# Who issues the 32 copies that double the keys: GpSimd, or ScalarE behind its weight conversions

## The reference

```python
q, kc, vc, ks, vs, kw, vw, gl = jnp.split(h @ w_in, splits, axis=-1)
kc, ks, kw = [partial_rope(to_heads(t, G), cos, sin) for t in (kc, ks, kw)]
# compressed branch: blocks of 32 tokens through a small MLP
return jax.nn.gelu(blk @ w1) @ w2            # once for kc, once for vc
# selected branch: softmax(q . ks) @ vs; window branch: softmax(q . kw) @ vw
o = gb[:, 0] * o_c + gb[:, 1] * o_s + gb[:, 2] * o_w
```

## Time and profile before

| | |
|---|---|
| median of 3 runs | 2381.58 us (2381.36 to 2381.64) |
| the profiled execution | 2382.09 us, of which its span is 2380.3 us |
| PE busy | 2370.0 us |
| PEld busy | 2002.1 us |
| DVE busy | 1332.7 us |
| ACT busy | 899.4 us |
| POOL busy | 310.5 us |
| mean granted TensorE clock | 0.999 |
| attention prologues (ACT's first copy of a high key half to the transposes on PE) | 53.5 to 113.5 us in layer 0, 1706.1 to 1772.3 us in layer 3 |

### The profile page before, as it was taken

The page is one execution under the profiler, slowest core; times in us unless marked ns, Lnnn a source line. Parts: engine busy times, 40 slices in busy tenths (PEclk is TensorE's granted clock), DMA queues, the critical chain, the costliest instruction groups (busy, mean ns, idle before and its releaser), DMA issues.

```text
span 2380.3 us, 33586 instructions
## 1 busy us (share of the span) xinstructions
PE 2370.0 (100%) x11768; PEld 2002.1 (84%) x11768; DVE 1332.7 (56%) x2199; ACT 899.4 (38%) x1376; POOL 310.5 (13%) x305
## 2 busy tenths in 40 slices
PE   9999999999999999999999999999999999999998
PEld 7899988888888888888888888888889998888887
DVE  8667765344465764443586644446756676534444
ACT  6267833222233432222233322223426773322223
POOL 2211140000040120000033000003420114000003
PEclk9999999999999999999999999999999999999999
DMA  4710023232233232322233223233370002223232
GB/s 165 224 46 2 2 69 108 88 101 93 99 105 106 89 106 91 103 97 97 97 99 106 97 91 104 89 106 105 121 208 27 2 2 89 97 89 106 89 105 89
DMA packets 64616, 220.58 MB, mean 93 GB/s; under 512 B 7680, under 2 KB 7808, under 8 KB 64512
## 3 DMA queue, kind: packets, MB, share of 16 engines
q1 hardware_dynamic: 58320, 208.59, 26.3%
q0 software_dynamic: 5184, 8.40, 1.6%
q10 hardware_dynamic: 1008, 2.21, 0.3%
HBM read 208.68 MB, written 2.10 MB: 89 GB/s over the span
## 4 chain that ended last, share of the span: by engine, by line
PE 99%; DVE 0%; DMA 0%; ACT 0%; SPq 0%; issue 0%; DVEq 0%
PE bank L1516 95%; PE bank L1796 3%; DMA x<-x_in 0%; PE bank L1826 0%; DVE branch L1281 0%; DVE big L1509 0%; SPq L434 0%; DVE rden L1276 0%; ACT L588 0%; DVE w_lo L939 0%; DVE rden L1278 0%; ACT w_hi L572 0%; PE bank L1700 0%; ACT xs_hi L581 0%; ACT xg L907 0%
## 5 line engine op out<-in xcount | busy, mean ns | idle before, releaser
L1516 PE MATMUL bank<-xs_hi,w_hi 128*128 128x512 f32 (+1 forms) x1808 | 708.9, 392 | 1.1 <-DVE xs_lo L947 0.5
L1516 PE MATMUL bank<-xs_lo,w_hi 128*128 128x512 f32 (+1 forms) x1808 | 703.3, 389 | 0.0
L1516 PE MATMUL bank<-xs_hi,w_lo 128*128 128x512 f32 x1792 | 697.3, 389 | 0.0
L939 DVE TENSOR_TENSOR w_lo<-raw,w_hi 128x1024 fp32r<-128x1024 f32 x369 | 469.7, 1276 | 230.7 <-ACT w_hi L572 226.3
L572 ACT ACTIVATE w_hi<-raw 128x1024 fp32r<-128x1024 f32 x372 | 390.8, 1051 | 432.6 <-PE bank L1516 231.7
L1516 PEld LDWEIGHTS bank<-xs_hi,w_hi 128*128 128x128 f32 (+1 forms) x1808 | 339.0, 188 | 74.4 <-DVE xs_lo L947 1.5
L1516 PEld LDWEIGHTS bank<-xs_lo,w_hi 128*128 128x128 f32 (+1 forms) x1808 | 338.4, 187 | 71.0 <-issue 1.0
L1516 PEld LDWEIGHTS bank<-xs_hi,w_lo 128*128 128x128 f32 x1792 | 336.4, 188 | 70.0
L1516 PE MATMUL bank<-hid_hi,w_hi 128*128 128x512 f32 x720 | 280.5, 390 | 0.0
L1516 PE MATMUL bank<-hid_lo,w_hi 128*128 128x512 f32 x720 | 280.1, 389 | 0.0
L1516 PE MATMUL bank<-hid_hi,w_lo 128*128 128x512 f32 x720 | 280.1, 389 | 0.0
(11 more groups left out here) (212 smaller groups left out, 2719.8 us busy)
## 6 DMA issues: line engine op xcount, KB each, us to landing
raw<-stream SPq DMA_DIRECT2D x371, 512.0 KB, 3.2
w_f<-stream SPq DMA_DIRECT2D x18, 512.0 KB, 3.5
hid_hi<-mix_hi POOLq DMA_DIRECT2D x32, 128.0 KB, 3.7
hid_lo<-mix_hi POOLq DMA_DIRECT2D x32, 128.0 KB, 3.1
out<-big SPq DMA_DIRECT2D x8, 256.0 KB, 2.9
x<-x_in ACTq DMA_DIRECT2D x4, 256.0 KB, 6.8
x<-x_in SPq DMA_DIRECT2D x4, 256.0 KB, 7.5
big<-consts SPq DMA_DIRECT2D x1, 664.0 KB, 11.0
```

The source lines that it names most:

```text
L939: nc.vector.tensor_tensor(w_lo[:, slot, :], raw[:, k, :], f32(w_hi[:, slot, :]), ALU.subtract).then_inc(w_lo_ready, counted(b))
L1516: return nc.tensor.matmul(out_, w, v, start=start, stop=stop)
```

## The change

The 32 copies of a layer leave POOL's list and go to ACT's. ACT issues them in its loop over blocks 8 to 23, four at a time, behind the conversion of that turn: for key tile i (0 to 3) the high half in turn j = 10 + 4i, the low half in j = 11 + 4i. The wait for the stage is kept; POOL's waits on `block_done`, which spaced its groups, have no successor. Source, destination (as float32 on both sides) and count of the copies are the same.

```diff
-                for j in range(KS, MIXED):
-                    for stage, key, ready in ((stage_hi, key_hi, stage_hi_ready), (stage_lo, key_lo, stage_lo_ready)):
-                        gp.wait_ge(ready, 4 * a + j - KS + 1)
-                        gp.wait_ge(block_done, plan.mix[l] + MIXED + 2 * (2 * (j - KS) + (stage is stage_lo)) - 2)
-                        for half in range(2):
-                            for h in range(2):
-                                gp.dma_start(key[64 * h:64 * h + 64, (j - KS) // 2, 2 * (j % 2) + half, :],
-                                             stage[64 * half:64 * half + 64, j - KS, :]).then_inc(key_full, 16)
...
+                def copies(j, stage, key, ready):
+
+                    act.wait_ge(ready, 4 * a + j - KS + 1)
+                    for half in range(2):
+                        for h in range(2):
+                            act.dma_start(f32(key[64 * h:64 * h + 64, (j - KS) // 2, 2 * (j % 2) + half, :]),
+                                          f32(stage[64 * half:64 * half + 64, j - KS, :])).then_inc(key_full, 16)
+
                 for j in range(MIXED, GATE):
                     split_after(B + j, (B + j) % RING)
                     if j < MIXED + 2:
                         post(j - 2)
+                    if (j - MIXED) % 4 == 2:
+                        copies(KS + (j - MIXED) // 4, stage_hi, key_hi, stage_hi_ready)
+                    if (j - MIXED) % 4 == 3:
+                        copies(KS + (j - MIXED) // 4, stage_lo, key_lo, stage_lo_ready)
                     if j == W1_AT[3] + 1:
                         hidden(0)
                     if j == W1_AT[3] + 4:
```

## The result

| | before | after |
|---|---|---|
| median | 2381.64 us (2381.26 to 2382.77, 20 runs) | 2385.47 us (2383.34 to 2390.97, 20 runs) |
| profiled execution | 2382.09 us | 2385.04 us |

The ratio is 1.0017, 95% interval 1.0011 to 1.0023. The kernel became slower by 3.8 us. That is inside 0.2%, but four times the loss of 0.9 us that was forecast (2382.5 us), and 0.3 us above the upper end of the range. Its runs also scatter more, 7.6 us against 1.5 us.

The account below looks back on a forecast made before the run. PE, busy 2370.0 of 2380.3 us, was taken as the bound. Waits of 0.77 us (layer 0) and 0.16 (layer 3), all else 0, gave 2382.09 + 0.93 = 2383.0 for the profiled execution, median 2382.5; range 2381.1 to 2385.2 us.

Parts of the forecast that it names:

- the place: Low half of key tile 3, between block 26's conversion and `hidden(1)`: PE waits 0.77 us in layer 0, 0.16 in layer 3.
- the three cases of the start: Group behind an ACTIVATE: issues start with it (taken), when it has ended (1.06 us later), or without waiting for its load.
- the rival of no stall: Deciding group issued while block 26's conversion still waits for its load; `hidden(1)` starts at 112.70 as before; 2381.6 us, chance 0.20.
- that of the late start: Deciding group waits for the ACTIVATE's end; PE loses 1.83 and 1.22 us, sum 3.05; 2384.6 us, chance 0.26.
- The other groups: Groups elsewhere in ACT's prologue list fall into its idle time, even eight issues behind block 21's conversion; cost 0.
- the last copies: Issued by about 113.6, landing at 117.1 to 121.0 against ACT's wait ahead of 120.47; worst case 0.5 us, not needed soon.
- The slower rival: Deciding group starts late and each issue costs ACT 0.70 us; 5.0 us lost, 2386.6 us, chance 0.07.
- the text's own signs of being wrong: PE waiting for `w_lo` or a score, layer 3's wait as long as layer 0's, or issues ahead of the conversion.
- The issue's price: Four copies on ACT: 0.34 us for the first, 0.50 for each other, 1.84 a group; ends 1.3 and 2.8.
- The copies' bytes: High half of tile 3, ahead of block 26's load: 0.5 MB need 1.4 us in a 2 us hole; cost 0.
- The range's upper end: 2385.2 us: the late start plus 0.6 us for a load that lands later.
- a loss of clock: TensorE's clock falling behind PE's stall would add time, but a stall of 2 us doesn't seem enough; no size given.

Follow-up runs that it names:

- high_behind: Changed kernel with the high half of key tile 3 issued behind `hidden(1)` instead of ahead of block 26's load; 2383.27 us, ratio 1.0006.
- eight: Changed kernel with the high half of key tile 3 moved to turn 23, so eight issues instead of four precede `hidden(1)`; 2389.94 us, ratio 1.0036.
- twelve: Changed kernel with twelve issues ahead of `hidden(1)` in turn 23: low half of tile 2, both halves of tile 3; 2398.06 us, ratio 1.0068.
- pool_late: Kernel before, copies on GpSimd, only the high half of key tile 3 issued later, behind the low half; 2381.85 us, ratio 1.0000.
- low_ahead: Changed kernel with the low half of key tile 3 ahead of block 26's conversion, right behind the high half; 2384.39 us, ratio 1.0012.
- pool_late_two: Kernel before, copies on GpSimd, both halves of key tile 3 issued late, when VectorE is done with block 24; 2384.21 us, ratio 1.0011.
- gelu_first: Changed kernel with `hidden(1)` ahead of turn 23's four copies, still behind block 26's conversion; 2382.24 us, ratio 0.9999.

## Why the prediction was right and wrong

Right were the place and one mechanism: the group between block 26's conversion and `hidden(1)`, with PE waiting for `tmp` twice and nowhere else in the two prologues. So was the choice among the three cases of the start: the issues begin with the ACTIVATE (111.99 and 111.98), not at its end and not while it waits for its load. With that the rival of no stall and that of the late start fell; the rule on the wait queue that stood behind the first, in the Trainium skill's page "Perfetto Trace Analysis", section "DVE / Act Engine Instruction (TENSOR_ADD, Activation, etc)", didn't hold for DMA issues behind a waiting ACTIVATE: the data of the copies had long been there, and the first issue still came only at the end of ACT's idle 7.72 us. The other groups cost nothing, as said; `hidden_turned(0)` and block 25 made nobody wait, and no wait is for the last copies. The slower rival's price of 0.70 an issue didn't hold either (0.62).

One of the text's own signs of being wrong nearly came: a wait in layer 3 as long as in layer 0. It had 0.16 against 0.77 us; measured were 1.48 and 1.64. The issues are the same in both layers, so what made the two alike is m, that is the load.

Three steps were off.

**The issue's price, a term mis-sized.** "I take 0.34 for the first of a group and 0.50 for each of three more, 1.84 us a group." The group in question took 2.42 and 2.41 us, 0.47 for its shortest issue and 0.62 for the median one. The nearest rows, loads from HBM on the same queue, were lower than the copies' price on ACT. POOL's for the very copies (0.52) were nearer, and even they too low. With the margins of before, 1.76 and 2.37, the need of 2.96 would make PE stand 1.20 and 0.59 us, 1.8 in all, where the text had 0.93. high_behind, with the same need and m of 2.25 and 2.46, measured 1.5 us above before. A smaller error hid part of this one, by luck: the text took the start of PE's weight load, 113.26, for the moment at which PE wants `hidden(1)`. The stalls fit the transposes' start, 113.49, less 0.05. By that the text's own 1.84 us a group would have given 0.59 us in layer 0 and nothing in layer 3.

**The copies' bytes, taken as 0.** This is the larger miss, and the step that failed: "there is a hole of 2 us for these 0.5 MB, and at the 381 GB/s of the full window they need 1.4. I take 0." 381 GB/s was the rate of the weights' loads. Where copies fill the DMA engines the traces show 194 GB/s at a share of 0.81 (before) and 213 at 0.94 (after), which makes 2.5 us of these 0.5 MB. And they are later than in that reckoning: the issues take 3.01 us, from 103.20 to 106.21. So they overlap SP's loads from 106.3 on. What that does to m, in the ten layers of the five profiled kernels with the high half there and in the ten of five without it (before, eight, high_behind, twelve and the kernel before with the GELU ahead):

| | m, us | mean |
|---|---|---|
| high half of tile 3 in turn 22, on ACT | 1.32, 1.48, 2.42, 1.12, 0.38, 2.00, 0.98, 2.06, 1.55, 1.89 | 1.52 |
| not there | 1.76, 2.37, 2.40, 2.53, 2.25, 2.46, 2.05, 2.41, 2.46, 2.56 | 2.33 |

So 0.8 us a layer, 1.6 us in all, from the profiles, and 1.9 to 2.3 us from the medians of the changed kernel and high_behind.

That it is the bytes can be counted in the traces: the packets of the copies' queue between SP's issue of block 25's load (106.31 in after) and block 26's conversion (111.98).

| kernels, both layers | SP's issue to the conversion, us | of the copies moved in it, MB |
|---|---|---|
| the five without the high half there | 4.4 to 5.2 | 0 |
| pool_late | 4.5 and 4.9 | 0.06 and 0.01 |
| the five with it | 4.6 to 6.6 | 0.10 to 0.43 |
| low_ahead and pool_late_two (both halves) | 6.3 to 7.3 | 0.53 to 0.59 |

GpSimd issues the copies in pool_late, pool_late_two and two of the five kernels of the first row, ScalarE in the others: the delay goes with the bytes and not with the issuing engine. For the high half alone there is no run in which GpSimd issues it where ACT does in the changed kernel, so there this count is the evidence. What else scatters the load's landing within a row stays open.

For the profiled execution itself both terms together give 2.96 - 1.32 and 2.96 - 1.48, that is 3.1 us, where the profiled times differ by 2.95: without its stall PE would have come to layer 0's transposes 0.19 us earlier than before. The prediction did see this term, but only as "some tenths".

**The scatter.** The range's upper end counted 0.6 us for a load that lands later. Once `hidden(1)` is late, every tenth of the load's scatter (m from 0.4 to 2.4) goes to the end, one for one; before, m of 1.76 against a need of 1.38 still hid most of it. That is why the changed kernel's runs spread more, and those with `hidden(1)` ahead of the load by only 0.7 us. It isn't enough for all of the 7.6 us: with the lowest m seen where the high half is in turn 22, 0.4, in both layers, the stalls are 5.2 us, some 2387 us, and three runs are at 2388.8 to 2391.0.

**What stays open.** The medians differ by 3.8 us, the profiled executions by 2.95. The prediction dismissed a loss of clock ("a stall of 2 us doesn't seem enough"). In the profiled execution that was right: the granted clock is 1.00 through both stalls (1.6 and 1.5 us). In the two of the 20 runs of after with the lowest mean clock, 0.998, the times were 2388.77 and 2390.97 us; with eight issues the runs at 0.998 and 0.997 took 2391.48 and 2393.03 against 2388 to 2390 for the others; with twelve every run is at 0.996 or 0.997, and the profile shows the fall. A clock that falls in some executions would account for the upper tail; but a third run of after, 2388.78 us, was at 0.999, and no profile of a run with four issues caught a fall. For the changed kernel this is argued, not shown.

## What to carry to other kernels

In this kernel a DMA issue wasn't free on an engine whose next instruction was wanted: look at what stands behind it in the list, and at what the instruction ahead of it waits for, since here the issues started only then. Price the transfer's issue and its rate from rows of the same kind of transfer, source and destination included, and check that the bytes are through before the next load that matters, whoever issues them. The repair here isn't the issuing engine but the order: a short step that depends on nothing late belongs ahead of the instruction that waits for a load, which brought the time back to that of before (2381.80 us) and took the scatter out.

## What the runs showed of the hardware beyond that

- ACT's issues ran beside an ACTIVATE that had started: two (1.12 us) behind a conversion of 1.06 us delayed the next ACTIVATE by 0.25 us. No issue started while the ACTIVATE ahead of it waited for data (111.99 against 111.98), but issues passed one that waited only for the engine (gelu_first: 113.23 against 114.10).
- A copy of 64 partitions x 512 from SBUF to SBUF took ACT 0.62 us to issue (median; up to 1.58), POOL 0.52; it landed after 3.6 us from ACT and 3.5 us from POOL (medians).
- At a share of the DMA engines near 1, windows filled mostly by such copies moved 208 and 213 GB/s (after, 1766 to 1768 and 106 to 108), windows of weights 360 to 399 GB/s (108 to 110 in after and in high_behind).
- A stall of PE of 3.1 us left the granted clock at 1.00 in the profiled execution with eight issues; one of 6.0 us let it fall to 0.50.
